# Building the chunk responses by selecting products on TensorE, and moving modulation blocks behind the response rounds

## What is computed

```
mod = silu(c) @ w + b          # c: 9 rows; w: 1024 x 16384 in all, 64 MB
bu  = einsum("blgp,gnp->blgn", uf, b_bar)            # 64 groups of 16 channels, 64 states
h   = associative_scan(h[t] = lam_bar * h[t-1] + bu[t])
y   = real(einsum("blgn,gpn->blgp", h, c_mat)) + d_skip * uf
z   = gelu(y);  a, g = split(z @ w_glu);  out = a * sigmoid(g)
```

## Time and profile before

| | |
|---|---|
| median of 3 runs | 3530.94 us |
| the profiled execution | 3527.4 us, of which its span is 3525.6 us |
| product of block 21, the last between the rounds, ends | 184.5 us |
| block 31's product starts | 259.06 us |
| first `y` round starts | 272.70 us |
| GLU products start | 313.02 us |

### The profile page before, as it was taken

The page is one execution under the profiler, slowest core; times in us unless marked ns, Lnnn a source line. Parts: engine busy times, 40 slices in busy tenths (PEclk is TensorE's granted clock), DMA queues, the critical chain, the costliest instruction groups (busy, mean ns, idle before and its releaser), DMA issues.

```text
span 3525.6 us, 62302 instructions
## 1 busy us (share of the span) xinstructions
PE 2587.8 (73%) x24981; PEld 949.6 (27%) x24981; DVE 2327.5 (66%) x5468; ACT 1234.7 (35%) x3842; POOL 1261.0 (36%) x1163
## 2 busy tenths in 40 slices
PE   4857997768667766667879997686686677666666
PEld 3735523204002300112225665040040023001000
DVE  8563686986775776465544444978767767775645
ACT  3312233343333333334433232343433343333333
POOL 0020233444443444424413511344444444443432
PEclk8868998769667877769999998696696678667666
DMA  8886799999999999999952157999999999999997
GB/s 292 302 283 258 291 406 407 414 411 407 419 417 418 401 419 420 402 413 399 406 180 92 38 199 300 413 399 421 420 402 417 420 420 407 420 419 398 415 421 317
DMA packets 192059, 1278.61 MB, mean 363 GB/s; under 512 B 30904, under 2 KB 36704, under 8 KB 44760
## 3 DMA queue, kind: packets, MB, share of 16 engines
q0 software_dynamic: 152912, 1112.35, 77.3%
q1 hardware_dynamic: 38288, 161.79, 12.7%
q10 hardware_dynamic: 576, 0.59, 0.1%
HBM read 1260.88 MB, written 11.40 MB: 361 GB/s over the span
## 4 chain that ended last, share of the span: by engine, by line
DMA 39%; PE 37%; DVE 16%; ACT 5%; issue 3%; POOL 0%; SPq 0%; ACTq 0%; DVEq 0%; PEldq 0%; POOLq 0%
DMA arena<-peer_uv,arena 35%; PE psum L2677 12%; DVE arena L2106 8%; PE psum L2622 6%; PE psum L2583 3%; DMA arena<-b_mod 2%; PE psum L3042 2%; PE psum L2756 1%; PE psum L2825 1%; PE psum L2469 1%; ACT arena L1397 1%; ACT arena L1394 1%; DVE arena L2024 1%; DVE arena L2117 1%; DVE arena L1679 1%
## 5 line engine op out<-in xcount | busy, mean ns | idle before, releaser
L2677 PE MATMUL psum<-arena 32*32 32x512 f32 x16384 | 1520.5, 815 | 743.9 <-ACT arena L1397 727.4
L1124 POOL DMA_INDIRECT arena<-peer_uv,arena x1040 | 1141.9, 1098 | 1825.8 <-PE psum L2677 1542.8
L2106 DVE SCALAR_TENSOR_TENSOR arena<-arena 128x1024 f32<-128x1024 f32 x1040 | 1273.4, 1226 | 757.3 <-DMA arena<-peer_uv,arena 740.0
L1384 ACT ACTIVATE arena<-arena 128x1 f32<-128x1 f32 x1040 | 210.4, 202 | 1551.0 <-DVE arena L2106 1550.1
L2677 PEld LDWEIGHTS psum<-arena 32*32 32x32 f32 x16384 | 216.0, 118 | 1907.5 <-ACT arena L1397 1783.5
L1397 ACT ACTIVATE arena<-arena 128x32 f32<-128x32 f32 x1024 | 329.1, 321 | 33.4
L1394 ACT ACTIVATE arena<-arena 128x1 f32<-128x1 f32 x1040 | 306.0, 294 | 33.8
L2622 PE MATMUL psum<-arena 128*128 128x128 f32 x2048 | 262.7, 285 | 14.8 <-DMA arena<-peer_wq 13.7
L2622 PEld LDWEIGHTS psum<-arena 128*128 128x128 f32 x2048 | 244.7, 197 | 83.6 <-issue 82.1
L2469 PE MATMUL psum<-arena 128*9 128x128 f32 x2048 | 87.5, 341 | 85.1 <-DMA arena<-b_mod 85.1
L2583 PE MATMUL psum<-arena 128*128 128x512 f32 x256 | 124.4, 618 | 2.9 <-DVE arena L1931 2.1
(11 more groups left out here) (341 smaller groups left out, 2292.3 us busy)
## 6 DMA issues: line engine op xcount, KB each, us to landing
arena<-w_mod SPq DMA_DIRECT2D x64, 1024.0 KB
arena<-peer_wq SPq DMA_DIRECT2D x12, 2048.0 KB
arena<-peer_uv,arena POOLq DMA_INDIRECT x1040
arena<-w_glu SPq DMA_DIRECT2D x5, 2048.0 KB, 12.3
arena<-mod_rows SPq DMA_DIRECT2D x4, 1024.0 KB
arena<-w_o SPq DMA_DIRECT2D x1, 4096.0 KB
arena<-mod_rows SPq DMA_DIRECT2D x7, 512.0 KB
arena<-x_after_layer SPq DMA_DIRECT2D x7, 512.0 KB
```

The lines of the kernel that those rows point to most:

```text
L1124: pool.indirect_dma_start(ring[r], None, a[f"peer_uv{t // 5}"], bass.IndirectOffsetOnAxis(ap=ix, axis=0)).then_inc(landed[r], 16)
L1384: act.activation(col, col, ACT.Gelu_apprx_tanh).then_inc(s_gl, 1)
L2106: dve.scalar_tensor_tensor(out=u, in0=u, scalar=1.0, in1=h, op0=ALU.mult, op1=ALU.mult, accum_out=at(DOTS + (t % 2) * 2 * P + m, 1)).then_ ...
L2677: ins = pe.matmul(acc_of(t, i, c), diag[rows, r, :], ring[r][rows, D + 512 * c:D + 512 * (c + 1)], start=(m == 0), stop=last, skip_group_c ...
```

## The change

`toep` is written by PE and ACT. Four new rounds `t` stand between the `k` and the `y` rounds. Round t_n takes 4 groups of each `ksb[r]` and, for each strip, multiplies it by a 16 x 32 selection matrix (an identity of 16 with 16 zero columns left or right of it), whose output lands in the partitions of that strip; an even and an odd strip share 32 partitions and add up in PSUM. The four r use four row tiles of the array and four banks. That is 32 products for a round, with 512, 448, ... 64 columns (four of each). ACT copies the result out in four pieces, each waiting for the one before. POOL clears only the parts that no copy writes, in three memsets, and issues no transfers.

Because the `t` rounds write `TOEP`, the blocks are dealt out anew. Six blocks stand in front, ten between the rounds (before: four and eighteen). Blocks 16 to 25 follow the last `k` round, in `MOD_PLACES[0]`, then comes t_0, and behind each of t_0, t_1 and t_2 two blocks in `MOD_PLACES[1]`; t_3 comes last. What waited for `s_toep` waits for ACT's copy of t_3.

```
-MOD_FIRST = 4
-MOD_ONE = 22
+MOD_FIRST = 6
+MOD_ROUNDS = 16
+MOD_ONE = 26
-                  + [("y", r) for r in range(NR)])
+                  + [("t", r) for r in range(NR)] + [("y", r) for r in range(NR)])
-        MOD_AFTER = [("m", 0), ("m", 1), ("m", 1), ("s", 0), ("u", 0), ("u", 1), ("u", 2), ("u", 3), ("u", 3), ("k", 0),
-                     ("m", 2), ("i", 1), ("k", 1), ("m", 3), ("i", 2), ("k", 2), ("i", 3), ("k", 3)]
+        MOD_AFTER = [("m", 0), ("m", 1), ("s", 0), ("u", 1), ("u", 3), ("k", 0), ("k", 1), ("i", 2), ("k", 2), ("k", 3)]
 # sync
-            sp.wait_ge(s_toep, 16 * TC * NR)
+            wait_copied(sp, ("t", NR - 1))
             sp.dma_start(hx[:, :, CH:CH + NB], a["state_x"]).then_inc(s_st0, 16)
 # gpsimd
-            pool.memset(at(TOEP, G * P), 0.0).then_inc(s_tz, 1)
-            pool.wait_ge(s_tz, 3)
-            for r in range(NR):
-                wait_copied(pool, ("k", r))
-                for s in range(TC):
-                    pool.dma_start(toep[GP * s:GP * (s + 1), RG * r:RG * (r + 1), GP * s:P],
-                                   ksb[r][:, :, 0:P - GP * s]).then_inc(s_toep, 16)
+            for c in range(1, 4):
+                pool.memset(toep[32 * c:32 * c + 32, :, 0:32 * c], 0.0).then_inc(s_tz, 1)
 # scalar
+            mod_evac(MOD_S5, MOD_FIRST)
+                if key == ("t", 0):
+                    mod_evac(MOD_ROUNDS, MOD_ONE)
+                    for b in range(2):
+                        act.wait_ge(s_modmm[b], MOD_ONE)
+                elif kind == "t":
+                    out = toep.rearrange("p (r g) m -> p r g m", r=NR)
+                    src = ps.rearrange("p r (g m) -> p r g m", g=4)
+                    for c in range(4):
+                        rows, t0 = slice(32 * c, 32 * c + 32), 32 * c
+                        ins = act.activation(out[rows, :, 4 * r:4 * r + 4, t0:P], src[rows, :, :, t0:P], ACT.Copy)
+                        if c < 3:
+                            link(ins)
+                if kind == "t" and MOD_ONE + 2 * r < NMB:
+                    for b in range(2):
+                        mod_copy(MOD_ONE // 2 + r, b)
-            mod_evac(MOD_ONE, NMB)
-            act.wait_ge(s_toep, 16 * TC * NR)
+            wait_copied(act, ("t", NR - 1))
 # tensor
+            def responses(ps, n_):
+                for c in range(4):
+                    for odd in range(2):
+                        t0 = GP * (2 * c + odd)
+                        for r in range(NR):
+                            out = ps[32 * c:32 * c + 32, r, :].rearrange("p (g m) -> p g m", g=4)
+                            ins = pe.matmul(out[:, :, t0:P], at(EYE - GP * odd, 32, 32 * r, 32 * r + GP),
+                                            ksb[r][:, 4 * n_:4 * n_ + 4, 0:P - t0], start=(odd == 0), stop=(odd == 1),
+                                            skip_group_check=True)
+                ins.then_inc(s_mm, 1)
+                if key == ("t", 0):
+                    wait_copied(pe, ("i", NR - 1))
+                    mod_products(MOD_ROUNDS, MOD_ONE, MOD_PLACES[0])
+                if kind == "t":
+                    responses(ps, r)
+                    if MOD_ONE + 2 * r < NMB:
+                        for b in range(2):
+                            mod_pair(MOD_PLACES[1])(MOD_ONE // 2 + r, b)
+                    continue
-                    wait_copied(pe, ("i", NR - 1))
-                    mod_products(MOD_ONE, NMB, MOD_PLACES[1])
-                    pe.wait_ge(s_toep, 16 * TC * NR)
+                    pe.wait_ge(s_tz, 5)
```

More of the change, by code:

```diff
@@ L92, in program @@
         SEL = o; o += NB
-        EYE = o; o += 32
+        EYE = o + GP; o += GP + 32
         SILU = o; o += KD * NC9
@@ L212, in program @@
         s_tz = sem("chunk_pad_and_response_cleared")
-        s_toep = sem("response_loaded")
         s_mm = sem("s5_round_products")
@@ L259, in program @@
                   + [("i", 0), ("k", 0), ("m", 2), ("i", 1), ("k", 1), ("m", 3), ("i", 2), ("k", 2), ("i", 3), ("k", 3)]
-                  + [("y", r) for r in range(NR)])
-        WHO = {"u": "A", "k": "A", "m": "A", "i": "V", "s": "A", "y": "V"}
-        MOD_AFTER = [("m", 0), ("m", 1), ("m", 1), ("s", 0), ("u", 0), ("u", 1), ("u", 2), ("u", 3), ("u", 3), ("k", 0),
-                     ("m", 2), ("i", 1), ("k", 1), ("m", 3), ("i", 2), ("k", 2), ("i", 3), ("k", 3)]
-        assert MOD_FIRST + len(MOD_AFTER) == MOD_ONE
+                  + [("t", r) for r in range(NR)] + [("y", r) for r in range(NR)])
+        WHO = {"u": "A", "k": "A", "m": "A", "i": "V", "s": "A", "t": "A", "y": "V"}
+        MOD_AFTER = [("m", 0), ("m", 1), ("s", 0), ("u", 1), ("u", 3), ("k", 0), ("k", 1), ("i", 2), ("k", 2), ("k", 3)]
+        assert MOD_FIRST + len(MOD_AFTER) == MOD_ROUNDS
         round_no = {key: n for n, key in enumerate(ROUNDS)}
@@ L767, in _ @@
             sp.dma_start(at(SILU, KD * NC9), a["c_t"]).then_inc(s_in, 16)
-            sp.dma_start(at(IDENT, P + TOPK + NB + 32), a["consts"]).then_inc(s_in, 16)
+            sp.dma_start(at(IDENT, P + TOPK + NB + GP + 32), a["consts"]).then_inc(s_in, 16)
             sp.dma_start(par, a["s5_par"][:, 0:NPAB]).then_inc(s_par, 16)
@@ L1915, in _ @@
             dve.wait_ge(s_modmm[1], NMB)
-            dve.wait_ge(s_toep, 16 * TC * NR)
+            wait_copied(dve, ("t", NR - 1))
             for gp in range(2):
@@ L3073, in host_inputs @@
     arr["consts"] = np.concatenate([np.eye(P), np.tile(np.arange(TOPK), (P, 1)),
-                                    np.arange(P)[:, None] // 16 == np.arange(NB)[None],
+                                    np.arange(P)[:, None] // 16 == np.arange(NB)[None], np.zeros((P, GP)),
                                     np.arange(P)[:, None] % 32 == np.arange(32)[None]], 1).astype(np.float32)
```

## The result

The changed kernel takes 3500.07 us (median of 4 runs, 3497.75 to 3505.28); the kernel before took 3530.72 us beside it (median of 4, 3525.8 to 3539.13). The ratio is 0.9913, with a 95% interval of 0.9891 to 0.9935: 30.7 us less. The profiled executions are 3527.4 us before and 3497.75 us after, their spans 3525.6 and 3495.6 us.

A forecast was written before the change was run, and what follows sets the result against it. DMA (39%) and PE (37%) held the chain, mostly in the experts; only the front would move. Copy of i_3 -21.6, then -1, block gaps +9.9, block 31 -1.8, tail +7.5: -7 us, giving 3524 us, range 3512 to 3543.

The forecast's parts named there:

- The step that failed: Expert layers: the change issues nothing there, so a shift of the first `y` round passes on to the end.
- Rival 4: Expert gathers start with shifted phases, so the front's gain is not seen at the end; a few us either sign, no chance given.
- the base: The one profiled execution the sum started from: first `y` round at 272.7 us, whole execution 3527.4 us.
- The copy of i_3: Last `i` round ahead of the late blocks: copied at 160 to 164 us, taken as 162, before 183.6.
- Block 17 at 169: First block waiting for its load behind the rounds: load issued at about 160 us, product starts 8.9 us later.
- Pitch of 5.4 us: Blocks 17 to 25: each costs 5.4 us once the transfers are gone, so block 25 starts at 212.3 us.
- The contention, 18.8 us: Blocks 22 to 27 before: response transfers slow weight loads, 45.8 us for five blocks, 18.8 us over 5.4 each.
- A `t` round of 4.2 us at full clock: New rounds on PE: 4.2 us each, between 3.1 and 4.6 by overlap of steps; 8.4 at half clock.
- Rival 3: `t` rounds on PE: 16-row tiles do not run side by side, 18.4 us a round, 3575 us in all; chance 0.03.
- Block 31 ends at 248.8: Last block, behind t_2: its load issued at about 237.5 us, its product from 246.4 to 248.8.
- The tail, 17 us: Block 31's end to first `y` round: t_3 4.2, ACT's copy 5.0, states 7.3; 7.5 us more than before.
- Rival 2: Last ten steps of blocks and `t` rounds: clock stays at 1.2 GHz, 17 us more, 3548 us; chance 0.12.

The follow-up runs named there:

- pad16: The kernel before with 16 unused words behind EYE, moving everything behind it, ring included, by 64 bytes to a multiple of 512: 3499.9 us, ratio 0.9921.
- ring16: The kernel before with 16 unused words right ahead of the gathers' ring, moving it and what lies behind or over it: 3499.4 us, ratio 0.9915.
- at256: The kernel before with everything behind STAT, ring included, moved 192 bytes down, to a multiple of 256 but not 512: 3498.6 us, ratio 0.9910.
- after_again: The changed kernel, unchanged, run and profiled a second time against the kernel before: 3508.9 us, ratio 0.9938.
- t_best: The changed kernel with six blocks in front, sixteen between the rounds, and the last `t` round ahead of blocks 24 to 31: 3476.1 us, ratio 0.9864.
- after_minus16: The changed kernel with ONES put at the arena's end, so the ring lies at its old byte 98752: 3533.4 us, ratio 1.0009 against the kernel before.
- new_deal_old_transfers: The kernel before with blocks dealt out anew (6, 10 and 16) and POOL's 32 transfers kept: 3536.9 us, ratio 1.0031.
- before_again: The kernel before, unchanged, run and profiled a second time as a control: 3523.0 us, ratio 1.0000.

## Why the prediction was wrong

**The step that failed** is the first one: "The change issues nothing there, so what it does to the start of the first `y` round" is "passed on to the end", with nothing else to count. The change does issue nothing in the expert layers, but it doesn't follow that it leaves them as they were. The price of that was put at nothing in the sum. A change that adds a word to a running sum of offsets moves every tensor behind it, and the gathers, 35% of the chain of waits by the page of before, write to one of them. pad16, ring16 and at256, in which nothing but places move, give 0.9921, 0.9915 and 0.9910; the change gives 0.9913, and 1.0009 with its ring back. So the placement is worth some 28 to 32 us by the ratios, the whole of the gain, and the rest of the change gains nothing. It rather costs: the 9 to 10 us between after_again and ring16 or at256, with `y_0` 11 to 12 us later. That the time fell, as was forecast, is luck: the forecast's reason, an earlier `y_0`, gave 0.9 us in the first pair of profiles and a loss beside all later ones of the old front. In no part of the sum, nor in a rival, was there a term for it. Rival 4 was near in place ("what is won ahead is not seen at the end") and wrong in kind.

The Trainium skill has the rule that I didn't weigh: page "DMA: Bandwidth & Descriptors", section "How a descriptor splits into AXI transactions", says that a descriptor's transfer is cut into transactions of 256 bytes that start at multiples of 256, so that one that starts between two multiples begins at the one below, and the bytes ahead of its start cost beats though nobody wants them. It tells of reading; here it is the written side that moved. The runs agree on the grain: multiples of 256 and 512 give the gain, 128, 64 and 32 don't. By that section's count, an estimate, 8192 bytes from 64 bytes ahead of a boundary are 262 beats instead of 256, 2.3% more. The packets measured less, 319.2 ns in mean against 315.5, 1.2%. The middle packet took 309 ns at a multiple of 256 or 512, 311 at one of 128, 312 at 64 and 313 at 32.

What the traces add is where such a percent lands. The gathers of both layers took 2743.6 us and take 2716.6, 1.0% less: the expert layers follow the gathers' rate nearly one to one. Over all the profiles of the table layer 1 is 1340 to 1350 us with the ring at a multiple of 32, 64 or 128 alone, and 1326 to 1330 at one of 256; the two groups don't touch. DVE's wait for gathers, in the row shown above, separates them too: 740 to 760 us and 710 to 726. Layer 0 alone doesn't (1397 to 1415 us and 1390 to 1401).

**The second step that failed** is the base. The sum was made on one execution whose front was unusually late: 272.7 us, where this front usually needs 260.7. The forecast for the changed front was 265.8, an early gain of 6.9 us; it came at 271.8, 6 us later than forecast and 11 us later than the usual front of before. How much of that reaches the end? From the start of `y_0` to the end of the span are 3249 to 3271 us in the seven profiles with the ring off a multiple of 256, and 3224 to 3241 in the seven with it at such a multiple. Within a group the figure doesn't follow an early or a late front: in the change it is 3223.8 us behind a `y_0` at 271.8 and 3241.3 behind one at 272.1, in t_best 3223.7 behind one at 245.2. So nothing shows that the layers take the front's loss back, and the 9 to 10 us of after_again fit a loss that is passed on whole. The spread of some 18 us within a group keeps any single pair from proving it; the 3 us of after_minus16 are within it.

**The terms of the front, one by one.**
- The copy of i_3 at 160 to 164 us, taken as 162: it was 163.1. Right. But the usual front of before is done at 168 to 176 us and not at 183.6, so the gain of 21.6 us is really some 5 to 13.
- Block 17 at 169: 169.8. Right.
- Pitch of 5.4 us: 5.7, from eight gaps of 45.95 us. Block 25 started at 215.7 instead of 212.3: 3.4 us late, most of it (2.7) from the mis-sized pitch, the rest from block 17. It is a mean over gaps of 5 and of 7 us, and the four gaps I had read it from were too few.
- The contention, 18.8 us: right. All gaps of about 9 us went with the transfers, and came back at another place in new_deal_old_transfers. In before_again, too, the five gaps from block 22 to block 27 take 46.1 us.
- A `t` round of 4.2 us at full clock: 2.6 us for the last three, at a granted clock of 1.00, and 4.7 for t_0, at 0.50. Row tiles with 16 rows ran side by side, and the even and odd strips too, below my lower bound of 3.1. Rival 3 is out.
- ACT's copy of a `t` round, 5.0 us: 5.01. Right.
- Block 31 ends at 248.8: at 256.1. 7.3 us late: 3.4 at block 25, 2.9 more between the `t` rounds, where the DMA share is only 0.86 (a load is issued when the block two earlier is half done, and a `t` round stands in between), and 1.0 since block 31's product ran mostly at the low clock (0.55 in its 3.3 us).
- The tail, 17 us: 15.7, from 256.1 to 271.8. t_3 and its copy are in it, as forecast.
- POOL's memsets, 10.4 us: 10.62, hidden. The row answers to the earlier trace rows, and it waited for block 25 as forecast:

```profile
220.02 10.62 POOL L1107 MEMSET arena<- 32x2048 f32 x3 [133.05 <-PE psum L2483]
```

- The sample state's transfer lands in 7.5 us (7.4 in the earlier trace rows), beside ACT's 7.50 us.
- Rival 2, a clock that stays at 0.50 through the last ten steps: it was 0.74 from 223.9 to 252.7 us, and three of the four `t` rounds ran at 1.00. Out.

So the front was right in its mechanism, and wrong in its balance: the transfers' contention went, and five blocks and a longer tail took its place, which came to more than it had cost. The split of the experiments says it plainly. On the usual front of 260.7 us the `t` rounds are worth -8 us (253.0), the new dealing +19 on top, of which some 6 are t_3 and its copy in the tail (15.7 us from block 31's end to `y_0`, where it was 9.5). It takes blocks from where they cost PE time beside the rounds (2.75 us each) and puts them where each costs a full load (5.7 us). t_best does the reverse and gains 15.5 us over the usual front of before.

## What to carry to other kernels

Where gathers of long rows bound a kernel, look at the start of their destination in a partition, and at what an edit does to it: put such buffers at a multiple of 256 bytes (the runs moved a gather's ring; plain loads were not tried), and when a change moves the layout, time the old kernel with that padding alone. Fold work in as long as the loads have room beside it: a block that streams while PE has other work costs its product only, and one behind that work costs its transfer. And profile the kernel before twice: a stretch of waits and bursts can differ by 15 us between two executions of one program, more than the change to be judged.

## What was not expected of the hardware

- An 8192-byte packet of an indirect gather took 309 ns in 95 to 97% of the cases when its destination started at a multiple of 256 bytes, in 45% at a multiple of 128, in about 24% at 64 or 32. That 45% were fast gave no time, since the mean packet was hardly shorter (318.7 ns against 319.2).
- Eight steps of four row tiles with 16 contracted rows and 32 columns, 32 products of 512 to 64 columns in f32, took 2.6 us at full clock.
- 32 transfers within SBUF, in runs of 512 to 64 bytes, go with a fall of the DMA rate from 363 to 285 GB/s beside 2 MB loads, and of the blocks' gaps from 5.7 us to 9.2 in mean and 10.6 at most.
- The granted clock over the same 105.8 us of one program was 0.78 in one execution and 0.91 in another.
